# A decoder layer with a routed mixture of experts: small work placed later, a finer last pair, routing by column blocks, an eleventh weight buffer used once

## The reference, cut to what matters

```
h = rmsnorm(x); proj = h @ w_in                      # 1024 x 2816
o_a, o_b, o_c, o_d = moba, differential, stick-breaking, sliding-window attention (4 heads each)
merged = sum_i sigmoid(h @ w_gate[i]) * (o_i @ w_br[i])   # w_gate[i] 1024 x 1024, w_br[i] 256 x 1024
x = x + merged @ w_o                                 # 1024 x 1024
h2 = rmsnorm(x)
group = argmax(h2 @ w_rg + b_rg) of 4; two experts of its 8 by h2 @ w_re + b_re
x = x + sum over the two: gate * ((silu(h2 @ w1[e]) * (h2 @ w3[e])) @ w2[e])   # 32 experts
out = rmsnorm(x)                                     # w1, w3 1024 x 512, w2 512 x 1024
```

## Time and profile before

| | |
|---|---|
| median of 3 runs | 717.75 us (717.66 to 717.78) |
| profiled execution, own time | 719.13 us |
| its span, first to last instruction | 717.3 us |
| PE busy | 685.7 us (96%) |
| DVE, ACT, POOL busy | 245.9, 192.0, 4.2 us |
| DMA | 243.56 MB, mean 340 GB/s |
| mean granted clock of TensorE | 0.990 |

### The profile page before, as it was taken

How to read it: one execution, slowest core, us unless ns; L and a number is a source line. 1 busy time by engine, 2 the same in 40 slices (tenths; PEclk the granted TensorE clock), 3 DMA queues, 4 the chain that set the end, 5 groups by cost and what they waited for, 6 DMA issues and landing times.

```text
span 717.3 us, 9888 instructions
## 1 busy us (share of the span) xinstructions
PE 685.7 (96%) x4042; PEld 401.6 (56%) x4042; DVE 245.9 (34%) x526; ACT 192.0 (27%) x304; POOL 4.2 (1%) x8
## 2 busy tenths in 40 slices
PE   8999999999999999999999999999989899898995
PEld 6899887777777874344344344344334343442432
DVE  7463556766567673121121121122121020210212
ACT  5551565598563521100100100001000010000112
POOL 0000000000000000000000000000000000000000
PEclk9999999999999999999999999999999999998998
DMA  8899631374439978999999999999999999999992
GB/s 308 284 273 286 215 117 59 118 259 152 176 118 343 406 307 292 409 428 426 426 427 426 425 428 426 429 426 428 428 429 426 429 427 428 424 428 429 414 399 104
DMA packets 46125, 243.56 MB, mean 340 GB/s; under 512 B 10192, under 2 KB 13448, under 8 KB 33800
## 3 DMA queue, kind: packets, MB, share of 16 engines
q1 hardware_dynamic: 45640, 241.45, 84.6%
q0 software_dynamic: 448, 1.59, 0.7%
HBM read 241.96 MB, written 1.07 MB: 339 GB/s over the span
## 4 chain that ended last, share of the span: by engine, by line
PE 63%; DMA 22%; SPq 6%; DVE 5%; ACT 2%; issue 2%; POOLq 0%; DVEq 0%; ACTq 0%
PE bank L1713 21%; DMA unit<-in_w 20%; PE bank L1768 8%; PE bank L1386 7%; PE bank L1387 7%; PE bank L1388 7%; SPq L548 5%; PE bank L1691 4%; DMA unit<-in_w_in 2%; DVE low L332 2%; PE bank L1780 1%; PE bank L1781 1%; PE bank L1742 1%; PE bank L1478 1%; ACT high L327 1%
## 5 line engine op out<-in xcount | busy, mean ns | idle before, releaser
L1713 PE MATMUL bank<-unit,xT 128*64 128x512 f32 x1024 | 230.8, 604 | 14.0 <-DMA unit<-in_w 12.3
L1713 PEld LDWEIGHTS bank<-unit,xT 128*64 128x64 f32 x1024 | 76.0, 139 | 153.5 <-issue 147.1
L1768 PE MATMUL bank<-unit,hidT 128*64 128x512 f32 x480 | 106.3, 595 | 0.0
L1386 PE MATMUL bank<-high,hT_hi 128*128 128x512 f32 (+2 forms) x208 | 79.8, 384 | 2.4 <-DVE low L332 2.4
L1387 PE MATMUL bank<-low,hT_hi 128*128 128x512 f32 (+2 forms) x208 | 77.3, 372 | 0.0
L332 DVE TENSOR_TENSOR low<-unit,high 128x2048 fp32r<-128x2048 f32 (+1 forms) x34 | 70.7, 2099 | 11.4 <-ACT high L327 11.4
L1768 PEld LDWEIGHTS bank<-unit,hidT 128*64 128x64 f32 x480 | 33.1, 137 | 61.5 <-issue 60.0
L1388 PE MATMUL bank<-high,hT_lo 128*128 128x512 f32 (+2 forms) x176 | 65.1, 370 | 0.0
L327 ACT ACTIVATE high<-unit 128x2048 fp32r<-128x2048 f32 (+1 forms) x34 | 58.9, 1756 | 8.4 <-PE bank L1388 5.1
L1263 DVE TENSOR_TENSOR y_lo<-bank,y_hi 128x512 fp32r<-128x512 f32 x30 | 20.7, 691 | 94.1 <-ACT y_hi L793 94.1
L1691 PEld LDWEIGHTS bank<-pick,hk 128*128 128x128 bf16 x768 | 44.4, 98 | 13.5 <-issue 12.2
(11 more groups left out here) (252 smaller groups left out, 688.0 us busy)
## 6 DMA issues: line engine op xcount, KB each, us to landing
unit<-in_w SPq DMA_DIRECT2D x86, 2048.0 KB, 30.1
unit<-in_w_gate SPq DMA_DIRECT2D x8, 2048.0 KB, 9.9
unit<-in_w SPq DMA_DIRECT2D x12, 1024.0 KB, 26.6
unit<-in_w SPq DMA_DIRECT2D x14, 512.0 KB, 9.0
unit<-in_w_in SPq DMA_DIRECT2D x3, 2048.0 KB, 15.9
unit<-in_w_br SPq DMA_DIRECT2D x4, 1024.0 KB, 6.0
unit<-in_w_o SPq DMA_DIRECT2D x2, 2048.0 KB, 10.6
unit<-in_w_in SPq DMA_DIRECT2D x6, 512.0 KB, 7.6
```

Source lines behind the costliest of these rows:

```text
L1386: mm(dst, a_hi, b_hi, start=first, stop=False)
L1713: last = mm(bank[4 + w][g * CAP:(g + 1) * CAP, :], xT[:, k, g * CAP:(g + 1) * CAP], rhs, start=(k == 0), stop=(k == KD - 1))
L1768: last = mm(bank[6 + n][g * CAP:(g + 1) * CAP, :], hidT[:, c, g * CAP:(g + 1) * CAP], rhs[:, c, n * BANK:(n + 1) * BANK], start=(c == 0), ...
```

## The change

Ring and loads: a unit `ONCE = 3` (pair 0's second w3 unit) has a buffer of its own, `unit_once`, over the place of x and of the low parts of the merged rows; x moves to lie next to them, and several small tiles move. All later units take the ring's turns one place earlier. Units 9 and 10 come in halves now, 11 and 12 in quarters, 13 on its own before the loop.

```diff
-HALVED = (8, 9)
+HALVED = (9, 10)
+ONCE = 3
+        units.append(place("unit_once", [P, UNIT], offset=x_at))
+        def turn_of(n):
+            return n if n < ONCE else n - 1
         def slot_of(n):
-            return EXPERT_SLOTS[n % RING]
+            return RING if n == ONCE else EXPERT_SLOTS[turn_of(n) % RING]
+        def occupant_ahead(n):
+            return n - RING - 1 if n - RING - 1 < ONCE else n - RING
             def load_expert_unit(n, i=0, loop=False):
-                if n < RING and not loop:
+                if n <= RING and not loop:
                     k = slot_of(n)
-                    if k < RING1:
+                    if n == ONCE:
+                        sp.wait_ge(s["absorbed"], 1)
+                        sp.wait_ge(s["squared2"], 2 * NT)
+                        sp.wait_ge(s["remains"], 2 * NT)
+                    elif k < RING1:
...
-                    sp.wait_ge(*free_of(n - RING, i))
+                    sp.wait_ge(*free_of(occupant_ahead(n), i))
...
+            load_expert_unit(ONCE)
             for quarter in range(4):
-                for n in (RING, RING + 1):
+                for n in (RING + 1, RING + 2):
...
+            load_expert_unit(RING + 3)
+            head = RING + 4
```

```diff
+                if u == 1:
+                    sp.dma_start(dst[:, 0:4, :], src[:, 0:4, :]).then_inc(s["second_half"], 16)
+                    dst, src = dst[:, 4:, :], src[:, 4:, :]
...
-            act.wait_ge(s["lamx"], 1)
-            nc.scalar.activation(lam[:, 2:4], lam[:, 0:2], ACT.Exp).then_inc(s["lame"], 1)
             for u in range(6):
...
+                if u == 3:
+                    act.wait_ge(s["lamx"], 1)
+                    nc.scalar.activation(lam[:, 2:4], lam[:, 0:2], ACT.Exp).then_inc(s["lame"], 1)
...
-            dve.wait_ge(s["small"], 16 * 9)
-            dve.wait_ge(s["table"], 1)
-            nc.vector.tensor_tensor(dvec[:], bank[7][0:12, 0:MAP], bmask[:], ALU.add).then_inc(s["dvec"], 1)
+            def bias_vectors():
+                dve.wait_ge(s["small"], 16 * 9)
+                dve.wait_ge(s["table"], 1)
+                nc.vector.tensor_tensor(dvec[:], bank[7][0:12, 0:MAP], bmask[:], ALU.add).then_inc(s["dvec"], 1)
+            def constants():
...
+            def weight_of_difference():
...
             for u in range(6):
                 for i in range(ends[u - 1] if u else 0, ends[u]):
                     if i % 2:
...
+                    if i == 5:
+                        bias_vectors()
                 for half in range(2 if u < 5 else 0):
                     low_part(dve, nc.vector, u + 2, half)
+                if u == 2:
+                    constants()
+                elif u == 3:
+                    weight_of_difference()
...
                 if st == 7:
+                    low_part(dve, nc.vector, 10, 1)
                     head_squares_summed()
-                if st == 7:
-                    low_part(dve, nc.vector, 10, 1)
                     head_norms_end()
```

```diff
-            for b in (0, 1, 4):
+            for b in (0, 1):
+                read_out(b)
             scores_ahead(0)
+            read_out(4)
...
+            branch(3, 3, [0])
             pe.wait_ge(s["mrg"], 14)
-            turn_tile(0, merged, s["mTps"])
-            branch(3, 3)
+            turn_tile(0)
+            branch(3, 3, [1])
...
             out_product(0, 1)
+            turn_rows(0, 0)
+            turn_rows(1, 0)
             out_product(1, 1, range(4))
-            pe.wait_ge(s["x1"], 3)
-            turn_tile(0, x, s["h2ps"])
+            turn_rows(0, 1)
             out_product(1, 1, range(4, KD))
-            route(0, range(4))
-            pe.wait_ge(s["x1"], 4)
-            turn_tile(1, x, s["h2ps"])
-            route(0, range(4, KD))
-            route(1)
+            route(0, range(4))
+            route(1, range(4))
+            turn_rows(1, 1)
+            route(0, range(4, KD))
+            route(1, range(4, KD))
+            for t, n in QUARTERS:
+                last = absorb(t, n)
+            last.then_inc(s["absorbed"], 1)
             pe.wait_ge(s["bf"], 2)
-            for t, n in ((0, 0), (0, 1), (1, 0)):
-                absorb(t, n)
-            for _ in range(20):
+            for _ in range(30):
                 mm(bank[7][:, 0:P], ones_bf[:], before_bf[:], start=True, stop=True)
             pe.wait_ge(s["asg"], 1)
...
-            absorb(1, 1).then_inc(s["absorbed"], 1)
+            for _ in range(16):
+                mm(bank[7][:, 0:P], ones_bf[:], before_bf[:], start=True, stop=True)
```

```diff
+LAST_PIECES = ((0, 0, 0, 0, 4), (0, 0, 0, 4, 8),
+               (0, 2, 0, 0, 2), (0, 2, 0, 2, 4), (0, 2, 0, 4, 6), (0, 2, 0, 6, 7), (0, 2, 0, 7, 8),
+               (0, 4, 0, 0, 2), (0, 4, 0, 2, 4), (0, 4, 1, 0, 2), (0, 4, 1, 2, 3), (0, 4, 1, 3, 4))
...
                     turn_picks(main, p)
+                    combine(main, p - 1, [0])
                     up(1, main, p, slots, here)
-                    combine(main, p - 1, [0])
-                    turn_hidden(main, p)
+                    turn_half(main, p, 0)
                     combine(main, p - 1, [1])
+                    turn_half(main, p, 1)
...
-            for t in range(NT):
-                for n in range(2):
-                    sp.wait_ge(*((s[("half0", "half1")[t]], 1) if n == 0 else (s["scaled"], t + 1)))
+            for t, n, ready, count in ((0, 1, s["scaled"], 1), (1, 0, s["half1"], 1), (1, 1, s["scaled"], 2), (0, 0, s["half0"], 1)):
```

More of the change, by code:

```diff
@@ L185, in hybrid_decoder_layer @@
         wo_lo = place("wo_lo", [P, KD, TOK], F32R, offset=shared)
+        h2T = [place(f"h2T{t}", [P, KD, TOK], offset=(hT_at, shared)[t]) for t in range(NT)]
         sig_at = at[0]
@@ L318, in high_part @@
                 act.wait_ge(first_pieces[piece], 16)
+            elif xi == 1 and piece == 0:
+                act.wait_ge(s["second_half"], 16)
             else:
@@ L782, in experts @@
                     link(nc.scalar.activation(warm, warm, ACT.Sqrt))
[L784 removed]
                 if not first:
                     act.wait_ge(z["Y"], 2 * p)
[L787 removed]
+                if last:
+                    for half, (ready, done) in enumerate(((s["last_half"], s["last_half"]), (z["hTp"], z["hT"]))):
+                        act.wait_ge(ready, 2 if half == 0 else p + 1)
+                        nc.scalar.activation(hidT[:, 2 * half:2 * half + 2, :].rearrange("p c q -> p (c q)"),
+                                             bank[4 + half][:, 0:TOK], ACT.Copy).then_inc(done, 1)
+                else:
+                    act.wait_ge(z["hTp"], p + 1)
+                    nc.scalar.activation(hidT[:].rearrange("p c q -> p (c q)"), bank[4][:], ACT.Copy).then_inc(z["hT"], 1)
                 if not first:
@@ L1245, in gathered, with hidden @@
                                     ALU.mult).then_inc(z["xT"], 1)
-            def hidden(z, p, first=False):
+            def hidden(z, p, first=False, last=False):
                 dve.wait_ge(z["sg"], p + 1)
@@ L1252, in hidden @@
                     dve.wait_ge(z["hTp"], p)
-                V.scalar_tensor_tensor(out=hid[:], in0=sg[:], scalar=slot_gate[:], in1=bank[5][:],
-                                       op0=ALU.mult, op1=ALU.mult).then_inc(z["hid"], 1)
+                if not last:
+                    V.scalar_tensor_tensor(out=hid[:], in0=sg[:], scalar=slot_gate[:], in1=bank[5][:],
+                                           op0=ALU.mult, op1=ALU.mult).then_inc(z["hid"], 1)
+                    return
+                for half, done in enumerate((s["last_half"], z["hid"])):
+                    of = lambda ap: ap.rearrange("p (q c) -> p q c", c=CE)[:, :, 2 * half:2 * half + 2]
+                    V.scalar_tensor_tensor(out=of(hid[:]), in0=of(sg[:]), scalar=slot_gate[:], in1=of(bank[5][:]),
+                                           op0=ALU.mult, op1=ALU.mult).then_inc(done, 1)
             def outputs(z, p, first=False):
@@ L1270, in experts @@
                     picks(main, p + 1, p + 1)
-                hidden(main, p, first)
+                hidden(main, p, first, last)
                 if not last:
@@ L1724, in turn_hidden, with turn_half @@
                 last.then_inc(z["hTp"], 1)
+            def turn_half(z, p, half):
+                pe.wait_ge(*((z["hid"], p + 1) if half else (s["last_half"], 1)))
+                for c in range(2):
+                    c_th = hid[:].rearrange("p (q c) -> p c q", c=CE)[:, 2 * half + c, :]
+                    last = nc.tensor.transpose(bank[4 + half][:, c * P:(c + 1) * P], c_th, ident)
+                last.then_inc(z["hTp"] if half else s["last_half"], 1)
             def turn_picks(z, p):
```

167 lines of the change are left out of this document (93 added, 74 removed).

## The result

The changed kernel takes 722.34 us in the median of 10 executions (720.29 to 725.99); the kernel before, beside it on the same chip, 717.76 (717.42 to 720.18). The ratio is 1.0061, 95% interval 1.0052 to 1.0071: 4.4 us slower. Forecast were 721.0 and 0.62 for slower. Two executions far outside the rest, 1164.72 us in e11 and 2439.52 of the kernel before beside e9 to e11, are left out of all medians and ratios. The profiled execution took 723.25 us, its span 721.5, 4.1 more than the span of before.

A forecast was written before the change was run, and what follows sets the result against it. PE was taken to bound the kernel until pair 0's down product ends (292.88 us), DMA to set the pace afterwards. Terms summed to 3.2 us slower: 722.3 profiled, 721.0 median; 8-in-10 range 715.0 to 723.2.

The forecast's parts named there:

- dvec stall: Ahead of block 7, PE waits for the later bias add, which stands behind unit 2's low parts: 2.7 us lost.
- break-even of 27.4: Landing time of unit 2 at which the later bias add neither gains nor loses; 30.17 was expected.
- Clock: After the idle time ahead of block 7, PE's granted clock falls: 2.2 us lost, between 1.7 and 2.8.
- Bank 4: Near 78 us, first scores run during the last block's copy, bank 4 being read out later: 0.6 us gained.
- Stage 7: Low part ahead of the head squares removes one wait but delays norms and stage 8: net 0.4 us lost.
- Branch product: Last branch product split in two, three products filling a wait ahead of 227.69: 0.25 us gained.
- Routing: Second logits earlier, positions and the gather of pair 0 sooner: 0.87 us gained, bounds -0.7 and 1.4.
- POOL's remainder: Routing's last remainder moved from DVE to POOL: taken as 1.8 us, hidden up to 3.5.
- Last pair: Final expert pair: moved combine half, earlier stores and finer pieces, together 0.35 us gained, bounds -0.5 and 1.
- the finer pieces: Last units loaded in smaller pieces in the last pair: no effect, 0.
- the stores: Final stores no longer queue behind POOL's half, the first going 0.9 us earlier: 0.6 us gained.
- Eleventh unit: Extra slot fills DMA's hole behind 264, but DMA idles later and unit 14 starts at the same event: gain 0.

The follow-up runs named there:

- e11: Changed kernel with small loads behind unit 2, bias add early, stage 7's old order, early release of pair 0's w2 halves: 712.69 us, ratio 0.9931.
- e9: Changed kernel with the twelve small loads queued behind unit 2's load, bias add still late: 717.47 us, ratio 0.9988.
- e2: Kernel before with only the bias add moved late, behind the copy of block 5: 721.92 us, ratio 1.0044.
- e1: Changed kernel with the bias add early again, ahead of unit 2's low parts: 715.19 us, ratio 0.9977.
- e3: Changed kernel without its eleventh slot, ten slots in a ring again: 723.00 us, ratio 1.0075.
- e4: Changed kernel with 20 fill products on TensorE in its wait ahead of block 7: 720.18 us, ratio 1.0036.
- e5: Changed kernel with the first half of pair 0's w2 slots released early, loads there in 2 KB pieces: 719.95 us, ratio 1.0035.
- e12: e11 with the routing's last transposes ahead of the second group of router products and 26 fill products: 712.31 us, ratio 0.9922.
- e8: e1 with stage 7's old order back, head squares ahead of the low part: 716.62 us, ratio 0.9981.
- e10: Kernel before with only stage 7's order changed, low part ahead of the head squares: 718.94 us, ratio 1.0014.
- e7: Changed kernel with bias add early, stage 7's old order, early w2 release, routing's last transposes earlier, 26 fill products: 712.98 us, ratio 0.9938.

## Why the prediction was right, and where not

*dvec stall, +2.7.* Right: e2 shows that the move does it, e1 that undoing it takes it back. 2.4 in the profile, since unit 2 landed at 29.8 and not at 30.2. I took one landing for a constant. In the changed kernel's relatives with the same front, ACT began unit 2 at 27.43, 28.27, 28.47 and 29.83, and PE stood 3.2 to 5.0 where nothing filled the wait; so the term is 0 to 2.4 (with e3's dvec block 7 starts at 34.71, and at the full clock block 8 would end when it did before), and part of the spread of 5.7 us is likely to come from here. The break-even of 27.4 held: e3's landing of 27.43 lost nothing by the wait itself, e9's of 25.43 gained.

*Clock, +2.2.* Right in kind, and in this profile 0.5 too small: 28 products times 0.095 is 2.66. But that is the dearest of four. At the full clock 42.8 us pass from block 7's start to the first scores (e4, 36.09 to 78.89); in the changed kernel it is 45.4, in e3 and e5 44.2 (34.71 to 78.93, 35.75 to 79.96), and in e2 44.3 without its wait of 0.56 for bank 4. So in these three the fall cost 1.4 to 1.5, less than the forecast's lower edge of 1.7. The fall itself came in all four profiles that have the wait, after 2.12 (e2), 3.16, 3.27 and 5.01 us, and e4, where only the idle time was filled, kept 1.00. At 5.01 the trace agrees with the Trainium skill's rule on idle gaps ("TensorE: Matmul & The Clock Gate", "Why this matters for your kernels"). Length alone does not decide, though: in the expert stage a wait of 3.75 us in e11 kept the full clock, as one did in e12, and one of 3.74 in e5 was followed by slow products:

```profile
619.24 7.09 PE L1797 MATMUL bank<-unit,xT 128*64 128x512 f32 x32 [3.75 <-DMA unit<-in_w]
```

```profile
653.72 8.78 PE L1797 MATMUL bank<-unit,xT 128*64 128x512 f32 x32 [3.74 <-DMA unit<-in_w]
```

*Bank 4, -0.6:* -0.64. *Stage 7, +0.4:* +0.43 by itself. What the step missed is that these three waits, 1.58 in sum, can bring the clock down: it fell behind them in 3 of the 7 profiles with this order (e1, e3, e4) and in none of the 7 without it, at 1.6 us each. *Branch product, -0.25:* -0.14.

*Routing, -0.87:* -0.29; the failed step. I let only "the fourth group, its weighting and eight small products" stand behind the output product's end. But PE runs its program in order: behind that end stand all 16 calls of the router product, 32 instructions, and four transposes, from 259.34 to 263.54 or 4.2 us, and the rows above show them without a gap. The kernel before had the same 32 there behind eight transposes: from the last addition to the second logits it took 4.61 us, now 4.11, and of this 0.50 the output product's end had lost 0.44. So the second logits came at 263.65, 4.61 later than before, where the transposes of the merged rows had come 4.67 later: a gain of 0.06 and not 1.39. What remains is the one DVE operation less, 0.23. POOL's remainder took 1.39, not 1.8, and hid; the Trainium skill's factor of two ("GPSIMD Engine Reference", "Performance versus the Vector engine") would have made it 2.14; the trace has a factor of 1.3 (1.39 against 1.07), so it does not agree here. And here too the clock can fall, behind the router's narrow products: in 4 of 10 profiles with the new routing (e4, e8, e11, e12), in none of the 4 with the old one, at 1.4 to 1.6 us.

*Last pair, -0.35:* -0.25, which is luck: two wrong terms cancel. I costed the finer pieces at 0; with them, from pair 0's combine to the last combine it is 407.4 to 407.6 in the six profiles without the early release (the changed kernel, e1, e3, e4, e8, e9), against 409.1 to 409.7 in the three of the old form (before, e2, e10): 1.6 won. It is not the eleventh slot, for e3 has it too (407.4). Which of it is the pieces and which the moved combine was not separated. And I costed the stores at -0.6; they go out 0.97 earlier, and yet the tail is 1.31 longer. SP's stores (DMA issues to landing, least, median, greatest us), first of before, then of after:

```profile
DMA to landing us min/median/max: 2.0/2.4/2.7
```

```profile
DMA to landing us min/median/max: 2.0/2.7/4.6
```

One of the four now takes 4.6 us; in all ten kernels with the new order of stores the slowest took 4.0 to 4.9, in all four with the old 2.7. In the DMA's slices it moves its last part at 10 to 31 GB/s for 2 us, where the old order moved 219 to 410 to the end. Why is open: the order of rows and columns, or its start beside POOL's end; no run took it alone, but it comes every time: from the last combine to the end it is 9.2 to 10.1 us in the ten, 8.5 in the four.

*Eleventh unit, 0.* Right, and by the mechanism told: empty ahead of unit 14, refilled by the end of the down product, same length from there (417.5 us with ten slots in e3, 417.4 with eleven).

In sum: +3.2 forecast, +4.1 in the profile. Of the 0.9 too little, 0.6 is the routing, 0.5 the clock behind the stall and 0.2 the branch product and the last pair, less 0.35 of stall. The median over executions holds, beside this, the falls in stage 8 and in the routing, and shorter stalls and shorter falls against them; how often each comes, no run counted. That the profile's 4.1 and the ratio's 4.4 lie so close is therefore partly luck: the first scores stood at 82.48 here, at 78.9 to 80.0 in the profiles of e3, e4 and e5, which have the same late bias add.

## What to carry to other kernels

Ask of an operation moved "to where it does not disturb" which transfer stands ahead of it in its engine's program, and who waits behind it; a wait of 2 us on TensorE was paid twice, once as the wait and once as slow products. A further buffer gained nothing here by itself (e3), as no release fell into the time that it won: look for the event that refills the queue. In a stretch in which an engine never waits, count every instruction of its program up to the result, since reordering them gave nothing here (e7).

## What the hardware showed unasked

The clock's falls come in some profiles and not in others with the same stretch, and between executions of one kernel the mean granted clock differs: in e1 the four executions with 0.992 or more took 714.5 to 715.1 us, the four with 0.988 or less 717.1 to 719.4. The changed kernel spread over 5.7 us and e8 over 2.0; the kernel before stayed within 1.5 in the 29 executions beside e5 to e8 (716.98 to 718.42), but spread over 3.1 and 3.5 beside the runs e1 to e4 and e9 to e11. Removing one occasion (e8) was followed by a fall at the next. With transfers cut into 2 KB pieces among the rest, a full share moved 8 to 15% less than 427 GB/s (e5). The slowest store's landing went from 2.7 to 4.6 us; its order and the moment of its start changed, and the last pair ahead of it, and none of these was taken alone.
